# A mixture-of-experts stage that gathers its tokens unnormalised: the norm factor goes into the pick matrix, one expert's weights of each odd quad get memory of their own

## The reference, cut to what matters

```python
def rms_norm(x, g):
    xf = x.astype(jnp.float32)
    xf = xf * lax.rsqrt(jnp.mean(xf * xf, axis=-1, keepdims=True) + NORM_EPS)
    return (xf * g.astype(jnp.float32)).astype(x.dtype)
...
        h = h + merged @ w_out[l]
        h = h + hier_moe(rms_norm(h, norm2_g[l]), w_router_group[l], b_router_group[l],
                         w_router_expert[l], b_router_expert[l], w_expert_in[l], w_expert_out[l])
    return rms_norm(h, norm_f_g)
```

## Time and profile before

| | us |
|---|---|
| median of 3 runs | 921.76 (921.53 to 922.46) |
| the profiled execution | 921.46 |
| its span | 919.6 |

### The profile page before, as it was taken

One profiled execution on the slowest core, in us unless ns is written; L12 is line 12 of the kernel. 1 busy time (PEld: TensorE's weight loads), 2 busy tenths in 40 slices (PEclk: granted clock), 3 DMA queues, 4 the chain that ended last, 5 costly groups with the idle time before them and its releaser, 6 DMA issues.

```text
span 919.6 us, 14705 instructions
## 1 busy us (share of the span) xinstructions
PE 833.9 (91%) x5971; PEld 692.2 (75%) x5971; DVE 494.2 (54%) x767; ACT 385.7 (42%) x526; POOL 99.4 (11%) x116
## 2 busy tenths in 40 slices
PE   4989999899999996866677899999998899999996
PEld 3989789799997532312332599999996799999995
DVE  5899577754564411100110476555677577667584
ACT  5333543456332321111110665465554366556462
POOL 3222000111000000000000401122180100000000
PEclk9999999999999998978898999999999999999998
DMA  8665555144689999999999995435536546646511
GB/s 280 224 193 183 184 184 184 40 161 167 219 336 396 384 422 422 422 422 422 422 421 410 277 187 186 161 115 184 131 145 204 185 138 212 198 139 226 183 46 46
DMA packets 93647, 217.55 MB, mean 237 GB/s; under 512 B 13919, under 2 KB 44765, under 8 KB 81305
## 3 DMA queue, kind: packets, MB, share of 16 engines
q1 hardware_dynamic: 92905, 215.32, 64.9%
q10 hardware_dynamic: 576, 1.18, 0.4%
q0 software_dynamic: 112, 0.30, 0.3%
HBM read 215.44 MB, written 1.34 MB: 236 GB/s over the span
## 4 chain that ended last, share of the span: by engine, by line
PE 75%; DMA 13%; DVE 7%; issue 2%; ACT 2%; SPq 1%; POOL 0%; DVEq 0%; ACTq 0%
PE ps L851 18%; PE ps L852 17%; PE ps L853 17%; DMA moe_ring<-in_w_expert_in 12%; PE ps L1274 6%; PE ps L1190 6%; DVE w_lo L1651 2%; PE ps L1222 1%; PE ps L1212 1%; PE ps L1006 1%; PE ps L1016 1%; PE ps L1162 1%; DMA h_tok<-in_x 1%; PE ps L1000 1%; DVE breg L1760 1%
## 5 line engine op out<-in xcount | busy, mean ns | idle before, releaser
L853 PE MATMUL ps<-x_hi,w_lo 128*128 128x256 f32 x664 | 189.2, 285 | 0.0
L853 PEld LDWEIGHTS ps<-x_hi,w_lo 128*128 128x128 f32 x664 | 128.8, 194 | 0.0
L1651 DVE TENSOR_TENSOR w_lo<-stage,w_hi 128x2048 fp32r<-128x2048 f32 (+1 forms) x44 | 101.9, 2354 | 25.2 <-ACT w_hi L1355 23.5
L851 PE MATMUL ps<-x_hi,w_hi 128*128 128x256 f32 x360 | 104.6, 291 | 9.1 <-DVE w_lo L1651 8.0
L852 PE MATMUL ps<-x_lo,w_hi 128*128 128x256 f32 x360 | 103.2, 287 | 0.0
L1355 ACT ACTIVATE w_hi<-stage 128x2048 fp32r<-128x2048 f32 (+1 forms) x44 | 79.1, 1849 | 54.5 <-PE ps L853 49.0
L851 PE MATMUL ps<-x_hi,w_odd 128*128 128x256 f32 x312 | 89.1, 285 | 1.3 <-DVE x_lo L1642 1.3
L853 PE MATMUL ps<-x_hi,w_odd 128*128 128x256 f32 x312 | 88.3, 283 | 0.0
L852 PE MATMUL ps<-x_lo,w_odd 128*128 128x256 f32 x312 | 88.3, 283 | 0.0
L851 PE MATMUL ps<-x_hi,w_lo 128*128 128x256 f32 x304 | 86.5, 285 | 0.0
L852 PE MATMUL ps<-x_lo,w_lo 128*128 128x256 f32 x304 | 86.0, 283 | 0.0
(11 more groups left out here) (387 smaller groups left out, 1918.8 us busy)
## 6 DMA issues: line engine op xcount, KB each, us to landing
stage<-in_w_in SPq DMA_DIRECT2D x23, 2048.0 KB, 8.7
moe_ring<-in_w_expert_in SPq DMA_DIRECT2D x44, 1024.0 KB, 18.1
moe_ring<-in_w_expert_out SPq DMA_DIRECT2D x20, 1024.0 KB, 16.1
stage_b<-in_w_up SPq DMA_DIRECT2D x12, 1024.0 KB, 7.6
stage<-in_w_down SPq DMA_DIRECT2D x11, 1024.0 KB, 5.0
stage<-in_w_up SPq DMA_DIRECT2D x10, 1024.0 KB, 9.5
up_odd<-in_w_expert_in SPq DMA_DIRECT2D x8, 1024.0 KB, 20.4
down_odd_a<-in_w_expert_out SPq DMA_DIRECT2D x6, 1024.0 KB, 20.8
```

What stands on the lines that cost most here:

```text
L851: mm(out, still[0], moving[0], start=first, stop=False)
L853: return mm(out, still[1], moving[0], start=False, stop=last)
L1651: tt(lo[:, cols], staged(n)[:, cols], hi[:, cols].bitcast(fp32), ALU.subtract).then_inc(lo_ready, 1)
```

## The change

- `pick_slots` makes `pick` as before and then, after a wait for it (`pick_made`), a second matrix `pick_x`: `pick` times the norm factor `rstd` of each token. The gathers have `h_tok`, at its step of four elements, as stationary operand, and `pick_x` as the moving one. `pick_gates` still reads `pick`.
- The four activations that wrote `xs_tok`, their semaphores and the two waits on PE go away.
- The memory of `xs_tok` holds `up_extra`: half 1 of expert j=0 ("lead") of the odd quads. So slot 1 of `moe_ring` has its part 0 for even quads alone. SP loads the lead of quad 1 ahead of `load_rest`, and after that the lead of quad q+2 right behind the three others of quad q+1. The last quad's lead lies in `up_extra` too; its other three still go to `up_last`. Two semaphores, `turn_in`, count the leads, and PE waits for one more of them at half 1.
- `h_tok` must now stay until the last gather, so `wide_g` moves to 176 KB (the first part of `down_odd_a`), and its DMA from ACT's queue, at L1484, to SP's, behind the wait for `y_b` and ahead of the `vvf` loads.

```diff
@@ -341,9 +341,10 @@
         y_tok = at_kib("y_tok", 104, [P, NT, D])
         y_junk = at_kib("y_junk", 112, [P, NT, D])
 
-        wide_g = at_kib("wide_g", 100, [P, D])
+        wide_g = at_kib("wide_g", 176, [P, D])
         choice = at_kib("choice", 192, [P, NT, D])
         mreg = at_kib("mreg", 168, [P, NT * D])
+        up_extra = at_kib("up_extra", 168, [P, KT // 2, UNIT])
         xs_tok = mreg[:, :].rearrange("p (t d) -> p t d", t=NT)
         junk = mreg[:, :].rearrange("p (t d) -> p t d", t=NT)
         merged = mreg[:, :].rearrange("p (f t) -> p f t", t=S)
@@ -420,6 +421,7 @@
         far = 4096.0
         pick = qk[:, 0:256].rearrange("p (t e c) -> p t e c", t=NT, e=QUAD)
         pick_gate = qk[:, 256:512].rearrange("p (t e c) -> p t e c", t=NT, e=QUAD)
+        pick_x = qk[:, 3584:3840].rearrange("p (t e c) -> p t e c", t=NT, e=QUAD)
         spread = qk[:, 512:768]
         xg = [qk[:, 768:1792].rearrange("p (k c) -> p k c", k=KT), at_kib("xg_odd", 198, [P, KT, P])]
         silu_g, act_tok = qk[:, 1792:2048], qk[:, 2048:2304]
...
@@ -472,7 +474,8 @@
 
         moe_in = [sem(f"moe_in{n}") for n in range(5)]
         up_last_in, down_last_in = sem("up_last_in"), sem("down_last_in")
-        pick_ready, gate_pick_ready = sem("pick_ready"), sem("gate_pick_ready")
+        turn_in = [sem("turn_in0"), sem("turn_in1")]
+        pick_made, pick_ready, gate_pick_ready = sem("pick_made"), sem("pick_ready"), sem("gate_pick_ready")
         gather_a, gather_b, spread_full, spread_ready = sem("gather_a"), sem("gather_b"), sem("spread_full"), sem("spread_ready")
         xg_a, xg_b, up_a, up_full = sem("xg_a"), sem("xg_b"), sem("up_a"), sem("up_full")
         silu_ready, act_ready, act_tr, actf_ready = sem("silu_ready"), sem("act_ready"), sem("act_tr"), sem("actf_ready")
@@ -604,6 +607,8 @@
 
         def expert_up(p, half, j, last=False):
 
+            if (p, half, j) == (1, 1, 0):
+                return up_extra[:, :, :]
             if last and half == 1:
                 return up_last[j]
             if (p, half) == (1, 0):
@@ -709,12 +714,19 @@
             w_up = a["w_expert_in"][0].rearrange("e (s p k) n -> s p e k n", s=2, p=P)
             w_down = a["w_expert_out"][0].rearrange("e (p f) n -> p e f n", p=P)
             low, high = range(0, 2), range(2, 4)
+            lead, others = range(0, 1), range(1, 4)
 
             def load_up(q, p, half, experts=range(QUAD), last=False):
                 for j in experts:
                     e = slice(q * QUAD + j, q * QUAD + j + 1) if isinstance(q, int) else bass.ds(q * QUAD + j, 1)
                     src = w_up[half][:, e, :, :].rearrange("p e k n -> p (e k n)")
-                    eng.dma_start(expert_up(p, half, j, last).rearrange("p k n -> p (k n)"), src).then_inc(up_last_in if last else moe_in[4 if (p, half) == (1, 0) else half], 16)
+                    if half == 1 and j == 0:
+                        landed = turn_in[p]
+                    elif last:
+                        landed = up_last_in
+                    else:
+                        landed = moe_in[4 if (p, half) == (1, 0) else half]
+                    eng.dma_start(expert_up(p, half, j, last).rearrange("p k n -> p (k n)"), src).then_inc(landed, 16)
 
             def load_down(q, p, experts=range(QUAD), last=False):
                 for j in experts:
@@ -728,7 +740,8 @@
                     eng.wait_ge(up_a, i * 2 + 1 + p + it0)
                     load_up(i * 2 + 2 + p, p, 0)
                     eng.wait_ge(up_full, i * 2 + 1 + p + it0)
-                    load_up(i * 2 + 1 + p, 1 - p, 1)
+                    load_up(i * 2 + 1 + p, 1 - p, 1, others)
+                    load_up(i * 2 + 2 + p, p, 1, lead)
                     eng.wait_ge(down_b, i * 2 + 1 + p + it0)
 
                 with eng.Fori(0, QUADS // 2 - 2) as i:
@@ -738,7 +751,7 @@
                 next_quad(QUADS // 2 - 2, 0)
                 load_down(QUADS - 2, 0)
                 next_quad(QUADS // 2 - 2, 1)
-                load_up(QUADS - 1, 1, 1, last=True)
+                load_up(QUADS - 1, 1, 1, others, last=True)
                 eng.wait_ge(up_full, QUADS - 1 + it0)
                 load_down(QUADS - 1, 1, last=True)
 
@@ -773,6 +786,8 @@
             eng.wait_ge(pj_full, units[units_one - 1]["read"])
             load_up(0, 0, 1, high)
             load_down(1, 1, range(2, 3))
+            eng.wait_ge(dve_split, 8)
+            load_up(1, 1, 1, lead)
             load_rest(0)
 
             eng.wait_ge(npass_ready, 1)
...
@@ -800,6 +816,7 @@
                         eng.dma_start(bias2[p:p + COPIES], skewed).then_inc(bias_in, 16)
                 if n == units_one:
                     eng.wait_ge(y_b, passes * QUADS)
+                    eng.dma_start(wide_g[:, :], a["norm_f_g"].unsqueeze(0).broadcast_to([P, D])).then_inc(normf_in, 16)
                 elif n == units_one + 1:
                     eng.wait_ge(up_a, passes * QUADS)
                 elif n > units_one + STAGES:
@@ -1076,9 +1093,8 @@
 
                 def gather_of(half, t):
                     for kk in range(4):
-                        k = 4 * half + kk
-                        last = mm(ps[:, half, kk * P:(kk + 1) * P], xs_tok[:, t, k * P:(k + 1) * P],
-                                  pick[:, t, :, :].rearrange("p e c -> p (e c)"), start=(t == 0 and kk == 0), stop=(t == 1),
+                        last = mm(ps[:, half, kk * P:(kk + 1) * P], interleaved(h_tok, t, half)[:, kk, :],
+                                  pick_x[:, t, :, :].rearrange("p e c -> p (e c)"), start=(t == 0 and kk == 0), stop=(t == 1),
                                   skip_group_check=True)
                     return last
 
@@ -1098,7 +1114,6 @@
                 router_logits(3, 1).then_inc(lg_full, 1)
 
                 eng.wait_ge(first_picked, 1)
-                eng.wait_ge(routed_xs, 1)
                 for half in range(2):
                     gather_of(half, 0)
 
...
@@ -1157,10 +1171,9 @@
                 eng.wait_ge(y_b, freed)
                 for half in range(2):
                     for kk in range(4):
-                        k = 4 * half + kk
                         for t in range(NT):
-                            last = mm(ps[:, half, kk * P:(kk + 1) * P], xs_tok[:, t, k * P:(k + 1) * P],
-                                      pick[:, t, :, :].rearrange("p e c -> p (e c)"), start=(t == 0), stop=(t == 1))
+                            last = mm(ps[:, half, kk * P:(kk + 1) * P], interleaved(h_tok, t, half)[:, kk, :],
+                                      pick_x[:, t, :, :].rearrange("p e c -> p (e c)"), start=(t == 0), stop=(t == 1))
                     last.then_inc((gather_a, gather_b)[half], 1)
 
             def quad(r, q, p, final=False):
@@ -1181,9 +1194,11 @@
                     if half == 0:
                         eng.wait_ge(moe_in[(0, 4)[p]], it * 32 + (64, 32)[p])
                     elif final:
-                        eng.wait_ge(up_last_in, r * 64 + 64)
+                        eng.wait_ge(up_last_in, r * 48 + 48)
                     else:
-                        eng.wait_ge(moe_in[1], r * (64 * (QUADS - 1)) + q * 64 + 64)
+                        eng.wait_ge(moe_in[1], r * (48 * (QUADS - 1)) + q * 48 + 48)
+                    if half == 1:
+                        eng.wait_ge(turn_in[p], it * 8 + (16, 8)[p])
                     for kk in range(4):
                         k = 4 * half + kk
                         for j in range(QUAD):
@@ -1468,20 +1483,11 @@
             def route():
 
                 half_square(1, 1)
-                for t in range(NT):
-                    eng.wait_ge(router_rstd, t + 1)
-                    for s in range(2):
-                        last = act(by_tile(xs_tok, t, s), interleaved(h_tok, t, s), ACT.Copy, scale=rstd[:, t:t + 1])
-                    last.then_inc(routed_xs, 1)
-
                 eng.wait_ge(gates_in, 1)
                 for t in range(NT):
                     act(weight[:, t, :], inside[:, t, :], ACT.Exp, bias=neg_v[:, t:t + 1]).then_inc(gates_exp, 1)
                     act(g_cell[1][:, t, :], lg[:, t, 0:GROUPS], ACT.Exp, bias=neg_g[:, t:t + 1],
                         accum_out=gsum[:, t:t + 1]).then_inc(gates_exp, 1)
-                eng.wait_ge(residual_in, 4)
-                eng.wait_ge(routed_xs, NT)
-                eng.dma_start(wide_g[:, :], a["norm_f_g"].unsqueeze(0).broadcast_to([P, D])).then_inc(normf_in, 16)
 
             def moe():
 
@@ -1800,7 +1806,6 @@
                 eng.wait_ge(router_pow, t + 1)
                 one = slice(t, t + 1)
                 newton(rstd[:, one], ms[:, one], nwt[:, one])
-                eng.sem_inc(router_rstd, 1)
 
             def choose(t, src, free):
 
@@ -1825,12 +1830,14 @@
                 step(ts(chosen[:, t, :], left[:, t, :], -2e38, None, ALU.is_le))
                 eng.sem_inc(sel_ready, 1)
 
-            def pick_slots(t, q):
+            def pick_slots(t, q, it):
 
```

(12 more changed lines are left out.)

1 line of the change is left out of this document (removed).

## The result

The changed kernel takes **925.33 us** (median of 7 runs, 923.61 to 927.83) beside 922.03 of the kernel before on the same chip (920.77 to 922.48): ratio 1.0043, interval 1.0032 to 1.0054. The forecast was 920.9, the range ended at 922.9. What came is the rival that I gave 0.07, the strided weight load, and its sign and place are as that rival had them (924.2); its working was not, as the part on the prediction shows.

The account below looks back on a forecast made before the run. The memory stream was taken to bound the experts' stage, up to quad 6's half 1 landing. A gain of 1.5 us there less 0.7 in the tail gave -0.8, so 920.9 us; range 919.0 to 922.9.

Parts of the forecast that it names:

- the strided weight load: Rival, chance 0.07: each load in route's gather takes 0.23 us more, route loses 3.7 us, kernel 2.4 us slower, 924.2.
- Bound and question: Experts' stage: the memory stream bounds it; the question is when the weights of quad 6's half 1 land, and what follows.
- Step 1, the lead: Transfer hole near 313 us: quad 1's lead ahead of it brings quad 6's landing up to 3.1 us earlier.
- Step 2, DVE: Route: DVE's added multiplications delay quad 0's half 0, +0.25 us before the router matmuls and +0.3 us before the gather.
- Step 3, the strided gather: Route's two gathers: reading `h_tok` at a step of four costs +0.03 us a load, +0.5 us in all.
- In the later quads the gather's extra microsecond lies beside waits of 20 us: Loop's later quads: the longer gather and DVE's two more operations lie beside PE's waits of 20 us and more.
- The landing: Quad 6's half 1 weights: forecast 1.5 us earlier; under the 0.07 rival, SP issues 3.2 us later, a loss of 1.7.
- Step 4, the tail: Behind the last quad: `wide_g` ahead of `vvf` lands the rest 1.3 us later; 0.7 us reach PE.
- The sum: Whole kernel: -1.5 at the landing plus 0.7 in the tail, -0.8 us; the 0.07 rival's total was 2.4 us slower.

Follow-up runs that it names:

- E1: The changed kernel with the gather's stationary operand contiguous in both places, features in the wrong order; 920.25 us, ratio 0.9986.
- E2: The kernel before with only the step of four added, in both gathers, read from `xs_tok`; 926.14 us, ratio 1.0053.
- V: The kernel before, keeping `xs_tok` and unscaled picks, with the odd quads' lead weights put where the tokens lie; 920.29 us, ratio 0.9988.
- V3: The kernel before with the odd quads' lead weights in the tokens' place and `wide_g` loaded whole in the tail; 919.83 us, ratio 0.9975.
- after: The changed kernel itself against the kernel before, here its first profiled execution; median 925.33 us, ratio 1.0043.
- A1: The changed kernel with no edit, a second profiled execution; 923.66 us in its one run.
- E4: The changed kernel with contiguous gathers and without DVE's norm factor, gathering through the unscaled `pick`; 920.55 us, ratio 0.9991.
- E9: The changed kernel with the contiguous gather in the route alone, the step of four kept in the loop; 921.58 us, ratio 1.0002.
- A2: The changed kernel with no edit, a third profiled execution; 925.92 us in its one run.
- E7: The kernel before with both gathers reading `xs_tok` at a step of two; 922.10 us, ratio 1.0003.
- E5: The changed kernel with ACT's split of `qka` in the tail moved behind the norm; 925.82 us, ratio 1.0048.

## Why the prediction was wrong, step by step

- **Bound and question: right.** (Slices 16 to 22 are 345 to 506 us, not 365 to 500; nothing hangs on it.) Memory bounds the quads, and the time hangs on half 1 of quad 6 and what lies behind. E1, E2 and V move with that landing.
- **Step 1, the lead: right in mechanism and about in size.** In E1, the change without the step of four, the loop's issue is 0.35 us later and half 1 of quad 6 starts 1.8 earlier. V, whose route is unchanged, starts it 2.45 us earlier with `wide_g` still in the route, V3 3.5 with it gone from there. I had 1.5 with 1.05 us of delay, and 3.1 as the upper end.
- **Step 2, DVE: right, in both places.** 0.25 + 0.3 was forecast. The first multiplication stands ahead of the yardstick's start: from the transposes of line 1091 (1074 before) to the router matmuls it is 1.24 us in after and A1 and 1.04 before and in E4, with PE idle for 0.22. The second is in the route: 0.35 longer in E1 (9.43 to 9.08), 0.25 of it the factor (E4). The row is 0.29 us.
- **Step 3, the strided gather: the step that failed.** I wrote 0.03 us for a load, 0.5 in the route. It measured 0.12 for a row (0.118 to 0.239), 2 us for each of the route's gathers, 2.9 on the route at full clock (A1's 12.35 against E1's 9.43: 1.0 from the first gather, since part of its two microseconds lies where PE idled for the ranks and for DVE, and 1.95 from the second) and 4.3 with the clock's fall. The error was to take the price from the transposes, the only rows with this step, and to pass over what I noted myself, that they are another kind of pass. They too show the step in the mean of a load: 207 ns for the strided ones of line 950 beside 141 for those of line 1031. But they keep a pace of 0.145, the gather's rows one of 0.239. Why a transposing pass gets by with less no run here tells. I cited the Trainium skill's rule of the lines, which spoke for a large price, and let the nearest row overrule it.
- **"In the later quads the gather's extra microsecond lies beside waits of 20 us": half wrong.** The waits begin at quad 2. Quads 0 and 1 have none, and there the 7.66 us delay `up_full` and open the second hole (E9: about 1.3 us).
- **The rival's number was in part luck.** It took 0.23 us for a load, twice what came, but counted one gather of 16 loads: 3.7 us on the route. Both gathers at that price, less the 0.6 us of idle time, make 6.8. The two slips nearly cancel: the measured 0.12 in both gathers is 2.9. So the price decides from 0.12 us for a load on, not from 0.2.
- **The landing.** The rival had SP 3.2 us later than the forecast, which is 4.25 later than before, and the landing 1.7 later. Measured in A1, with the clock up: issue 3.3 later, half 1 of quad 6 1.2 later; the 0.2 ahead of the yardstick comes to both.
- **Step 4, the tail: 0.7 forecast, 0, 0.3 and 1.45 measured** in A2, A1 and the first profile. The mechanism is there: against line 1160, the norm's transposes (1146 before), ACT's split starts 0.6, 1.0 and 2.2 us later than before the change, where 1.3 was forecast.
- **The sum.** A1 has neither of the clock's falls: half 1 of quad 6 +1.2, its 32 matmuls 6.39 us instead of 5.75 +0.6, PE's wait +0.3; together 2.2, and its span is 2.3 longer. The rival's 2.4 is the same total from other terms: it had 1.7 for the landing, 0.7 for the tail and nothing for the 32 matmuls. What lifts the median to 3.3 above is, as far as the profiles show it, the clock: A2, with the fall in the route, spends 1.4 us more there than A1, and of the seven runs of the changed kernel the three fastest have mean clocks of 0.984 and 0.981, the two slowest 0.977 and 0.974. The first profile needs 17.25 us from the second block's first matmul to line 1041 (542.97), A1 14.47, with the clock at 0.51 from 525 to 532 in the first. Whether the longer wait ahead of that fall caused it stays open: E1 waited 1.99 us and had none.

## What to carry to other kernels

Before TensorE's stationary operand is read at a step, look at the step: two fp32 were nearly free in this gather, four and eight doubled the row. By the Trainium skill's rule of the lines, cited at E7, the count to look at is how many elements fall in one 16-byte line, two or one. The transposes paid less at the same step (0.111 to 0.145 us), so a price read from another kind of instruction is a bound on neither side; where a rule speaks for a large price and the nearest row for hardly any, the range has to hold both. And memory for a prefetch can often be had without touching the work: V takes a place that is free just when the hole begins, and gets the gain without the price.

## What the runs showed of the hardware that I had not expected

- **The stair in the price of a stationary operand's step**: 192, 196, 329 and 334 ns for a load at steps of one, two, four and eight fp32.
- **The strided gather does not go by TensorE's clock.** Chain of A2, with the clock at 0.50 from 306 to 312:

```profile
303.73 3.91 PE ps L1096 x16
...
309.19 1.87 PE ps L1091 x2
311.05 3.59 PE ps L1096 x16
```

  The two contiguous rows of line 1091 take 1.87 us where they take 0.94 at full clock. The strided rows at 303.73 lie inside the fall for two microseconds, those at 311.05 for one. The clearest pair is the first gather of the changed kernel's first profile, where the clock is 0.59, 0.50 and 0.50 in the three microseconds from 303, and that of A1 at full clock:

```profile
302.57 3.91 PE ps L1096 x16
```
```profile
302.58 3.81 PE ps L1096 x16
```

  That fits a gather that waits for memory, not for the array. It does not prove it: a contiguous row, 0.118 us at full clock, would take 0.236 at half, by this estimate as long as the strided row's 0.239 at either level, and no profile has a contiguous gather in a fall.
- **A fall of the clock in the route, which had none.** In the kernel before PE idles 0.61 us at 304.75 between the first gather and the ranks; with the strided gather it is busy without a gap from the router matmuls on (4.00 of 4.00 us in 303 to 307), and in 5 of 8 profiles the granted clock then went to 0.50, the level of 1.2 GHz, for 3 to 7 us. With the fall the route was 0.2 to 1.4 us longer (12.57 and 13.72 beside A1's 12.35). Why it came in five and not in A1, E2 and E5 no run here tells.
